# Order of a unit's expert gathers: both heads of a token group in turn, with one spread for two dots

## What is computed

```
act = gelu(einsum('thkd,td->thk', u[eidx], hb))
y   = einsum('thk,thkd->td', wts * act, v[eidx])
```

## Time and profile before

| | us (counts and clock apart) |
|---|---|
| three runs | 1061.52, 1062.86 (median), 1063.50 |
| the profiled execution | 1062.72 |
| its span, first to last instruction | 1060.4 |
| first gather issued | 317.6 |
| first dot | 338.0 |
| last dot | 1046.3 |
| PE, DVE, ACT, POOL busy in the span | 841.2, 596.0, 363.5, 295.4 |
| PE matmuls and weight loads, each | 4660 |
| mean granted TensorE clock | 0.82 of 2.4 GHz |

### The profile page before, as it was taken

How to read it: one execution, slowest core, us unless ns; L and a number is a source line. 1 busy time by engine, 2 the same in 40 slices (tenths; PEclk the granted TensorE clock), 3 DMA queues, 4 the chain that set the end, 5 groups by cost and what they waited for, 6 DMA issues and landing times.

```text
span 1060.4 us, 13823 instructions
## 1 busy us (share of the span) xinstructions
PE 841.2 (79%) x4660; PEld 424.4 (40%) x4660; DVE 596.0 (56%) x1472; ACT 363.5 (34%) x1140; POOL 295.4 (28%) x319
## 2 busy tenths in 40 slices
PE   5999899999886787787786787777667766787684
PEld 4677777767534342343342332222222222222221
DVE  2032234332273999999799887455544454455444
ACT  2131322200123434536644434333433333333333
POOL 3100000000105334343334333333333333333330
PEclk9999889999997988986898867667776688667865
DMA  9742211225508999999999999999999999999993
GB/s 324 232 147 80 80 34 47 80 79 170 212 1 327 386 411 417 426 426 426 426 425 427 426 426 427 425 427 428 423 427 426 426 426 427 426 428 426 425 427 117
DMA packets 70762, 343.24 MB, mean 324 GB/s; under 512 B 8947, under 2 KB 22358, under 8 KB 33814
## 3 DMA queue, kind: packets, MB, share of 16 engines
q0 software_dynamic: 42496, 306.68, 69.2%
q1 hardware_dynamic: 28198, 35.70, 10.4%
HBM read 339.83 MB, written 3.54 MB: 324 GB/s over the span
## 4 chain that ended last, share of the span: by engine, by line
DMA 39%; PE 21%; DVE 12%; issue 9%; ACT 3%; POOL 0%; DVEq 0%; POOLq 0%; SPq 0%; ACTq 0%
DMA uv<-in_peer_uv,idx 37%; PE ps L539 4%; DVE uv L1653 4%; PE ps L914 3%; PE ps L895 3%; PE ps L857 2%; PE ps L753 2%; PE ps L759 1%; PE ps L775 1%; DMA wq<-in_w_peer_q 1%; DVE pick L1577 1%; DVE pick L1580 1%; DVE eij L1582 1%; PE ps L767 1%; PE ps L734 1%
## 5 line engine op out<-in xcount | busy, mean ns | idle before, releaser
L1653 DVE CUSTOM_DVE_ANT_0 uv<-ps,uv 128x1024 f32<-128x1024 f32 x288 | 351.4, 1222 | 219.3 <-DMA uv<-in_peer_uv,idx 192.4
L487 POOL DMA_INDIRECT uv<-in_peer_uv,idx x288 | 274.0, 951 | 464.6 <-PE ps L914 394.2
L895 PE MATMUL ps<-hl,e 128*128 128x512 f32 x512 | 245.2, 569 | 130.6 <-DVE dots L1653 130.2
L914 PE MATMUL ps<-uv,wz 128*32 128x256 f32 x2304 | 238.8, 496 | 27.6 <-ACT wz L1138 27.1
L895 PEld LDWEIGHTS ps<-hl,e 128*128 128x128 f32 x512 | 99.2, 242 | 286.3 <-DVE dots L1653 267.7
L1131 ACT ACTIVATE acts<-dots 128x1 f32<-128x1 f32 x288 | 58.5, 203 | 403.4 <-DVE dots L1653 401.5
L539 PE MATMUL ps<-hT,ring 128*128 128x288 f32 (+2 forms) x528 | 134.6, 412 | 0.0
L914 PEld LDWEIGHTS ps<-uv,wz 128*32 128x32 f32 x2304 | 51.2, 123 | 178.9 <-ACT wz L1138 162.1
L539 PEld LDWEIGHTS ps<-hT,ring 128*128 128x128 f32 (+1 forms) x528 | 97.8, 187 | 31.5 <-issue 3.3
L1138 ACT ACTIVATE wz<-cst,acts 128x32 f32<-128x32 f32 x288 | 93.0, 323 | 9.3
L1135 ACT ACTIVATE acts<-acts,wT 128x1 f32<-128x1 f32 x288 | 85.4, 296 | 9.4
(11 more groups left out here) (300 smaller groups left out, 743.3 us busy)
## 6 DMA issues: line engine op xcount, KB each, us to landing
ring<-in_w_in SPq DMA_DIRECT2D x6, 2048.0 KB, 10.1
ring<-in_w_in SPq DMA_DIRECT2D x5, 1024.0 KB, 5.3
uv<-in_peer_uv,idx POOLq DMA_INDIRECT x288, 15.1
ring<-in_w_out SPq DMA_DIRECT2D x2, 2048.0 KB, 8.1
ring<-in_w_branch_a SPq DMA_DIRECT2D x8, 256.0 KB, 6.3
ring<-in_w_branch_b SPq DMA_DIRECT2D x4, 512.0 KB, 6.9
ring<-in_w_peer_q SPq DMA_DIRECT2D x1, 2048.0 KB, 8.7
wq<-in_w_peer_q SPq DMA_DIRECT2D x1, 2048.0 KB, 13.5
```

The costliest lines, as they stand in the source:

```text
L487: pool.indirect_dma_start(uv[s][:, :], None, peer_uv, bass.IndirectOffsetOnAxis(ap=idx[:, u, at:at + 1], axis=0)).then_inc(uv_landed[s], 16)
L895: ins = pe.matmul(out, e8[:, v, :], rows[:, cols], start=True, stop=True)
L914: ins = pe.matmul(ps[32 * c:32 * c + 32, bank, c0:c0 + 256], wz[s][:, :], uv[s][:, D + 256 * c:D + 256 * c + 256], start=opens, stop=True, ...
L1653: dve.tensor_tensor_reduce(u, rows, u, 1.0, 0.0, ALU.mult, ALU.add, dots[:, s:s + 1]).then_inc(dotted, 1)
```

## The change

Within a unit the order of the gathers changes. A new function `pick_of(q)` gives token group and head for each q: in units of A and B the two heads of token group 0, then the two of group 1, and so on; in unit 0 eight gathers in a row that need the same spread. A spread is then made once for two dots (eight in unit 0), `SPREADS` lists the q at which one starts (0, 8, 16, 24, 32, 34, 36 ...), and `SPREAD_OF[q]` is the number of the spread that dot q reads. Spread k uses the pair of banks k % 2 and waits for all dots of spread k - 2. On PE only spread 0 is made ahead; the others stand ahead of combine q when q + 2 starts one. POOL and ACT read column 16 * head + group of the same lists. The sums are the same, added in another order.

```diff
--- before.py
+++ after.py
@@ -155,6 +155,20 @@
 TILE_OF = (C, A, A, A, A, B, B, B, B)
 NQ = N_UNITS * GROUPS
 SUM_BANK = {C: 4, A: 6, B: 4}
+
+
+def pick_of(q):
+
+
+    i = q % GROUPS
+    if TILE_OF[q // GROUPS] == C:
+        return i // 8 + 4 * (i % 8 // 2), i % 2
+    return i // 2, i % 2
+
+
+SHARED = [8 if TILE_OF[q // GROUPS] == C else 2 for q in range(NQ)]
+SPREADS = [q for q in range(NQ) if q % GROUPS % SHARED[q] == 0]
+SPREAD_OF = [sum(p <= q for p in SPREADS) - 1 for q in range(NQ)]
 
 
 def prepare_at(n):
@@ -483,7 +497,8 @@
                     pool.wait_ge(combined, q - NS + 1)
 
                 pool.sem_inc(pool_turn, 1)
-                at = q % GROUPS
+                g, w = pick_of(q)
+                at = 16 * w + g
                 pool.indirect_dma_start(uv[s][:, :], None, peer_uv,
                                         bass.IndirectOffsetOnAxis(ap=idx[:, u, at:at + 1], axis=0)
                                         ).then_inc(uv_landed[s], 16)
@@ -881,26 +896,27 @@
             need(pe, DRAINS["v"][-1], DRAINS["a"][-1])
             pe.wait_ge(e8_ready, 1)
 
-            def spread_rows(q):
-
-                t, g = TILE_OF[q // GROUPS], q % 16
+            def spread_rows(k):
+
+                q = SPREADS[k]
+                t, g = TILE_OF[q // GROUPS], pick_of(q)[0]
                 rows, v = (hlc[:, :], g % 4) if t == C else (hl[:, t, g // 8, :], g % 8)
-                if q % GROUPS == 0 and q // GROUPS in (0, 1, 5):
+                if q in (0, GROUPS, 5 * GROUPS):
                     pe.wait_ge(h2_split, ORDER.index(t) + 1)
-                if q >= 2:
-                    pe.wait_ge(dotted, q - 1)
+                if k >= 2:
+                    pe.wait_ge(dotted, SPREADS[k - 1])
                 for n in range(2):
                     cols = slice(512 * n, 512 * n + 512)
-                    out = ps[:, 2 * (q % 2) + n, :]
-                    ins = pe.matmul(out, e8[:, v, :], rows[:, cols], start=True, stop=True)
+                    ins = pe.matmul(ps[:, 2 * (k % 2) + n, :], e8[:, v, :], rows[:, cols], start=True, stop=True)
                 ins.then_inc(spread, 1)
 
             def combine(q):
 
-                u, g, s = q // GROUPS, q % 16, q % NS
+                u, s = q // GROUPS, q % NS
+                g, w = pick_of(q)
                 t = TILE_OF[u]
                 part = 0 if t == C else g // 4
-                opens = q % GROUPS < 16 and TILE_OF.index(t) == u and g % (16 if t == C else 8) == 0
+                opens = w == 0 and TILE_OF.index(t) == u and g % (16 if t == C else 8) == 0
                 if q == 32:
                     work_need(pe, "pq3")
                     work_need(pe, "list2")
@@ -938,11 +954,10 @@
                     ins = pe.matmul(out[:, 0:QUARTERS[t]], C_("quad"), fst[:, t, 0, 0:QUARTERS[t]], start=True, stop=True)
                 ins.then_inc(work_filled, 1)
 
-            for q in range(2):
-                spread_rows(q)
+            spread_rows(0)
             for q in range(NQ):
-                if q + 2 < NQ:
-                    spread_rows(q + 2)
+                if q + 2 in SPREADS:
+                    spread_rows(SPREADS.index(q + 2))
                 combine(q)
                 if q == 36:
                     pe.wait_ge(acc_read, 1)
@@ -1123,14 +1138,15 @@
 
             def weigh(q):
 
-                u, g, s = q // GROUPS, q % 16, q % NS
-                at = q % GROUPS
+                u, s = q // GROUPS, q % NS
+                g, w = pick_of(q)
+                at = 16 * w + g
                 act.wait_ge(dotted, q + 1)
                 if q >= NS:
                     act.wait_ge(combined, q - NS + 1)
                 act.activation(acts[:, 0, s:s + 1], dots[:, s:s + 1], ACT.Gelu).then_inc(gelu_done, 1)
                 act.wait_ge(gelu_done, q + 1)
-                if at == 0:
+                if q % GROUPS == 0:
                     act.wait_ge(weights_listed, u + 1)
                 act.activation(acts[:, 1, s:s + 1], acts[:, 0, s:s + 1], ACT.Copy, scale=wT[:, u, at:at + 1]
                                ).then_inc(factored, 1)
@@ -1646,9 +1662,10 @@
             def dot(q):
 
                 s = q % NS
-                dve.wait_ge(spread, q + 1)
+                dve.wait_ge(spread, SPREAD_OF[q] + 1)
                 dve.wait_ge(uv_landed[s], 16 * (q // NS + 1))
-                rows = ps[:, 2 * (q % 2):2 * (q % 2) + 2, :]
+                half = 2 * (SPREAD_OF[q] % 2)
+                rows = ps[:, half:half + 2, :]
                 u = uv[s][:, 0:D].rearrange("p (a b) -> p a b", a=2)
                 dve.tensor_tensor_reduce(u, rows, u, 1.0, 0.0, ALU.mult, ALU.add, dots[:, s:s + 1]).then_inc(dotted, 1)
```

## The result

The changed kernel took 1064.82 us (median of 17 runs, 1062.57 to 1065.84), the kernel before 1062.46 (17 runs beside it): ratio 1.0022, 95% interval 1.0014 to 1.0030. That is 2.4 us slower, 1.5 to 3.2 by the interval. The execution profiled took 1065.84 us, at the upper end of its runs, with a span of 1064.3.

What follows compares the result with a forecast made beforehand. Bound: 288 DMA gathers of 1 MB at 2.45 us each once queued; only the ramp before can move the end. Sum: +1.1 (gather 29) - 0.1 (code loading) = +1.0 on 1062.72, giving 1063.7 us; range 1060.5 to 1066.8.

Steps and rivals of the forecast that it cites:

- The clock: PE between projection bursts: low clock (1.2 GHz), so each burst starts cold; mean near 0.55 over 500-1020, from 0.75.
- The bursts: Two bursts of 32 projection matmuls on PE in the ramp: 5.8 us each instead of 3.84, ends 5.18 and 6.47.
- Dot 8: DVE, behind the first projection burst: starts at 356.34 against 355.25, making DVE 1.1 us late.
- Gather 29: POOL, behind the second projection burst: issued 2.9 us late, slack 1.8, so 1.1 us passes through.
- Gather 13: POOL, behind the first projection burst: issued 1.76 us late, hidden by 2.5 of slack (8.2 over 5.7).
- Gather 24: Gather of 383-384: late by DVE's 1.1 us, slack 1.0, so 0.1, taken in by gather 29's larger delay.
- No cost from the order, the columns or the late stage: Changed order waits for no later list: 0; after 500 about 9 us of queue cover hides a slower PE.
- instruction packets: Code loading on the instruction queue: two or three packets fewer of 37, worth -0.1 us, at most -0.9.
- The slower one: No slack at gather 29, all its delay passes: 1065.5 us, up to 1066.8; chance 0.30.
- The faster one: PE's clock stays high at the ramp's bursts, gather 29 gains 1.8 us: 1060.8, at best 1059; chance 0.20.

Runs made afterwards that it cites:

- the repeated half: Kernel before with half of its first projection burst (16 matmuls behind combine 4) made twice: 1063.99 us, +2.2, ratio 1.0027.
- the order alone: Changed kernel's new gather order, but a spread for every dot as in the kernel before: 1061.30 us, -0.7 against the kernel before.
- tiles A and B alone: Changed kernel with one spread for two dots in tiles A and B, but one per dot in the sample tile: 1061.91 us, -0.1 against the kernel before.
- repeated spreads: Changed kernel with a spread repeated into its own banks wherever the change left one out: 1062.23 us, ratio 0.9998 to the kernel before.
- the cut bursts: First two projection bursts cut into four pieces of 8 matmuls each: 1061.63 us on the kernel before, 1061.61 on the changed kernel.
- the first burst twice: Kernel before with the 32 projection matmuls behind combine 4 made twice: 1065.75 us, +2.9.

## Why the prediction was right, and where it was off

Forecast 1063.7, measured 1064.82: 1.0 us over the profiled execution before was forecast, 2.4 over the kernel before was measured. The direction and the mechanism held, from the clock to the late gathers; the slack that was to hide most of their delay was sized wrongly.

- **The clock.** Right. 0.58 over 500-1020 for 0.55 forecast. In the ramp it did not fall: up to the first burst it never rose. These are the windows of 340-344, kernel before and kernel after:

```profile
340.00:344.00 4.00, 3.06 (x22) 0.91 (x20) 4.00 (x18) 1.54 (x7) 1.38 (x2) 0.95 0.40 127
```
```profile
340.00:344.00 4.00, 2.16 (x16) 0.40 (x16) 4.00 (x18) 1.53 (x7) 0.96 (x1) 0.50 0.35 150
```

  With the spreads PE was busy for 3.06 of 4 us and had 0.95 of full speed; without them 2.16 and 0.50, its level in 336-340 in both kernels, and 0.50 again in 344-348. PE's idle stretches between the combines there are 0.83 to 1.11 us. The Trainium skill ("TensorE: Matmul & The Clock Gate", section "Why this matters for your kernels") has a row for either side: work without a break to come to the high clock, and no long gaps to keep it. The prediction weighed the second; the first is the one that applied ahead of the first burst, and this trace agrees with it. Nor were the gaps as short as the prediction took them to be: they reach 2.95 us in 364-384 in the kernel after, where the granted clock was 0.52.
- **The bursts.** Right: 5.8 forecast, 6.04 and 5.05 measured. Dot 8 was forecast for 356.34 and came at 357.03, 356.70 less the later dot 0. Gather 29 was forecast 2.9 late and was 2.6 late.
- **Gather 13: the step that failed.** "8.2 us, 2.5 of slack over 5.7: hidden." It went out 2.2 late, near the 1.76 forecast, but about 1.1 us of that had come through by gather 20, where the sum has nothing. So its slack was about 1.1, not 2.5. Part of the error is the reading: gather 13 itself took 7.7 us before, not 8.2. The larger part is that the 5.7 of one landing was taken for a floor that any landing may shrink to.
- **Gather 24.** "... slack 1.0, and is late by DVE's 1.1: 0.1". It was 1.2 late and added 0.1, but not for that reason: the gathers ahead were already landing 1.1 late. Issued 1.9 late, in the repeated half, it landed 1.9 late: the slack of 1.0 was not there either.
- **Gather 29.** Its slack of 1.8 was taken off the whole 2.9, DVE's 1.1 included, which left 1.1. With gather 29 and what follows late and nothing ahead of it, 1.5 us were hidden by the medians, within 0.4 to 2.2, and 0.8 by gather 36 of the profiled execution. In the kernel after the traces show nothing hidden: it went out 2.6 late, and gather 36 lands 2.9 late as a mean. By the last of its landings gather 29 came 3.5 us later, counted from dot 0, more than its issue was late. But this execution is among the longest of its 17, so how much of its own delay passed in the usual run stays open; the 2.4 measured is 1.5 to 3.2 by the interval.
- **No cost from the order, the columns or the late stage.** Right: the order alone and tiles A and B alone are within the measurement of the kernel before. 35 instruction packets for 37: two fewer, as forecast.
- **The rivals.** The slower one gave the time more nearly, 1065.5, and its sign came (374 GB/s in 384-404, gather 29 over 2 us late), but its reason, no slack at gather 29, is only half of what the runs show: some was there when gather 29 alone was late, none was seen behind gathers that were late already. The faster one needed a high clock at the bursts; when this was made with repeated spreads, the time was that of the kernel before, not 1.8 below it: gather 29 went out only 0.7 us earlier.

## What to carry to other kernels

Where an engine is busy without a break and the queue behind it is not yet full, lateness passes from one piece of work to the next, and here most of it came out at the end. The slack of the DMA is not to be read off one landing. Before work is taken off an engine that is not the bound, ask which later work of that engine *is* on the chain, and at which clock it will then start; here 28 spreads less in the sample tile made two bursts 2.2 and 1.2 us longer. A long burst in front of work that another engine waits for can be cut into pieces; here that repaired the loss, while a gain for the kernel before is not shown.

## What the runs showed of the hardware

- Spare PE work paid for itself: with 4656 matmuls on the page, for 4348 in the kernel after and 4660 in the kernel before, the first burst went from 6.04 to 3.84 us.
- The sixteen landings of one gather drift apart over the stage. In the kernel before the last landing of gather 36 comes 2.4 us after the first, that of gather 287 9.2 us after. The end is set by the last, so an earlier mean or first landing in the ramp, as with the cut bursts, need not be seen there.
- The start of the stage moves from one execution to another. In the profiled execution of the kernel with the first burst twice, dot 0 came at 330.81 us for 337.97 before, and the run took 1058.91 us where the median of that kernel is 1065.75. A single profiled time says little of a change of 2 us. Counted from dot 0 it says more: there the last landing of gather 287 is 4.1 us later than before, on the side of the median's 2.9, though not equal to it.
